# A ring of weights grows from two rounds of experts to three, and each engine reads the number of extra rounds earlier

## The chip, the cores and the metric

The kernel runs on one core of a Trainium2 chip. Its time is the device time of one execution in microseconds (us). All arithmetic is in float32. TensorE (PE) multiplies, VectorE (DVE), ScalarE (ACT) and GpSimd (POOL) do the rest, and SyncE (SP) issues the loads of the weights.

## The reference, cut to what matters

Two blocks run one after the other on 256 tokens of width 1,024. The first is one hybrid layer (three kinds of attention, then experts of hidden width 512); the second is two layers of another kind with experts of hidden width 256. Each of the three layers ends in a routed mixture: 32 experts in 4 groups, each token goes to 2 of them.

```python
x, xc = hybrid_layer(x, xc, ...)           # attention part, then hier_moe: 32 experts, 1024 -> 2*512 -> 1024
x = rms_norm(x, final_g)
for l in range(2):
    x = hybrid_layer_2(x, ...)             # mixers, then hier_moe_2: 32 experts, 1024 -> 2*256 -> 1024
out = rms_norm_2(x, final_g_2)

# an expert, for the tokens that chose it
g, u = split(h @ w_up[e]); y = (silu(g) * u) @ w_down[e]
```

The weights of the experts are 6 MiB for each expert of the first layer and 3 MiB for each of the others, so that 192, 96 and 96 MiB are read once; this is nearly all of the memory traffic.

## The kernel before, in words

**Stages.** A dense part (modulation, projections, attention, out-projection, norm, router) is followed by an expert stage, three times: stage 1 for the first layer, stages 2 and 3 for the layers 0 and 1 of the second block. Each engine has one program in order, and semaphores tie them together.

**Rounds.** An expert stage is a run of rounds. A main round takes one expert in stage 1 (32 rounds) and two in stages 2 and 3 (16 rounds each), with at most 32 tokens for an expert. An expert with more tokens has extra rounds ahead of its main round; they use the same weights, and only the main round gives the weights' memory back. How many there are depends on the routing, so it is a number in SBUF (`extra`), which every engine reads into a register (`value_load`, L913). `each_round` (L905) holds the loop. On TensorE one turn of it has two rounds, each with a body for an extra round (skipped by a branch when there is none, L914) and a body for the main round; on ScalarE and VectorE a turn has one.

A round on TensorE is, in this order: turn the gates (L965), up-projection (`up`, L987 in stage 1, L999 later; 64 matmul instructions), gather the tokens of the next round (L947), combine the result of the last one (`combine`, L974), transpose the hidden values (L1038), give slots back (L1041), transpose the gathered tokens (L954), down-projection (`down`, L1017 or L1010), and after a main round wait for its end and give back the other slots (L1049). ScalarE applies SiLU (L1077), copies the gathered tokens (L1071), the hidden values (L1080) and the result (L1082). VectorE marks the tokens of the next round (L1137, L1107), multiplies (L1142), and copies (L1146, L1126).

**Ring.** Weights arrive in a ring of `RING = 12` slots of 1 MiB (2,048 floats on each of 128 partitions). A round has `ROUND = 6` pieces: four of the up-projection and two of the down-projection. Dense layers use the same ring with pieces that take two slots each. TensorE counts used slots in `piece_used`; SP waits for the count before it loads a slot again (`expert_loads`, L446 to L461), in the order of use:

```python
sp.wait_ge(sems["piece_used"], turn * len(sources) + (base + j - RING + 1))
...
sp.dma_start(dst, src).then_inc(sem, 16)
```

So ahead of a stage two rounds can be in the ring.

**The other memory.** The activations of the dense layers lie in `arena` (18,944 columns) and in `hT` (4,096). The semaphore `mixed` says that all mixers of a layer have finished; the out-projection, the norm and the router follow it. The table `const2` of the second block is loaded once by POOL (L1192), after `fin_x`, the end of the first block.

Of the kernel before, what the change touches and what calls it, by code (L numbers as in the profile page):

```python
# [16 lines left out]
I32 = mybir.dt.int32  # L17
ALU = mybir.AluOpType
# [3 lines left out]
P = 128  # L22
# [5 lines left out]
RING = 12  # L28
ROUND = 6
NE = 32  # L30
# [125 lines left out]
SEMS = """params loaded_x loaded_ctx loaded_bias bias_out piece0 piece1 piece2 piece3 piece4 piece5 piece6 piece7 piece8 piece9 piece10 piece11 piece_used  # L156
# [42 lines left out]

class Ring:  # L200


    def __init__(self, sems):
        self.sems, self.n, self.loads = sems, 0, [0] * RING

    def place(self, dmas):

        slot = self.n % RING
        self.n += 2
        self.loads[slot] += 16 * dmas  # L210
        return slot, self.sems[f"piece{slot}"], self.loads[slot]

    def loop(self, turns, per_turn):

        out = []
        for j in range(per_turn):
            slot = (self.n + j) % RING
            out.append((slot, self.sems[f"piece{slot}"], self.loads[slot] + 16 * (j // RING + 1)))
        step = 16 * (per_turn // RING)
        self.loads = [n + step * turns for n in self.loads]  # L220
        self.n += turns * per_turn
        return out, step
# [20 lines left out]
def hybrid_kernel(nc, ins, out):  # L243
# [6 lines left out]
    with ExitStack() as ctx:  # L250
# [5 lines left out]

        ring = sb("ring", RING * SLOT).rearrange("p (r n) -> p r n", r=RING)

# [6 lines left out]
        hTf = sb("hT", KD * 2 * S)  # L265
        hT = hTf.rearrange("p (k n) -> p k n", k=KD)
        h2T = hTf[:, 0:KD * S].rearrange("p (k n) -> p k n", k=KD)
# [18 lines left out]
        arena = sb("arena", 18944)  # L286
# [7 lines left out]
        cxf = area(2048)  # L294
        rotf = area(1536)
        cx = cxf.rearrange("p (t d) -> p t d", t=NT)
        rot_b, rot_o = rotf[:, 0:512], rotf[:, 512:1536].rearrange("p (b n) -> p b n", b=2)
        qk = arena[:, 0:3584].rearrange("p (d n) -> p d n", d=2)
        q_pad = rotf[:, 0:512].rearrange("p (b m n) -> p b m n", b=2, m=2)
        probs1 = cxf.rearrange("p (b m n) -> p b m n", b=2, m=2)  # L300
        qaT = area(1024).rearrange("p (h n) -> p h n", h=4)
        kaT = area(2048).rearrange("p (h n) -> p h n", h=4)
        va = area(2048).rearrange("p (t n) -> p t n", t=4)
        vbn = area(2048).rearrange("p (t n) -> p t n", t=4)
# [4 lines left out]
        rT = area(512).rearrange("p (h n) -> p h n", h=2)  # L309
        glow = area(512)  # L310
        nb_biasf = area(2048)
        nb_bias = nb_biasf.rearrange("p (t h n) -> p t h n", t=2, h=4)
        const1 = area(n_c1)
        C1 = {n: const1[:, a:a + w] for n, (a, w) in c1.items()}
        mixf = area(2048)
        mixT = mixf.rearrange("p (k n) -> p k n", k=KD)
        wdec = area(256)[0:32, :].rearrange("p (d n) -> p d n", d=2)
# [18 lines left out]
        band_flat = arena[0:GRID, 3584:7168]  # L336
        band = band_flat.rearrange("p (r u) -> p r u", u=P)

        work = arena[:, 0:3584]
# [8 lines left out]
        junk = arena[:, 3584:4608]  # L348
        router_w = kaT.rearrange("p h n -> p (h n)")[:, 0:288].rearrange("p (k n) -> p k n", k=KD)
        rt = kaT.rearrange("p h n -> p (h n)")[:, 288:2048]  # L350
# [9 lines left out]
        extra = ctx.enter_context(nc.sbuf_tensor("extra", [1, NE], I32))  # L360
        zeros = rt[:, 960:1088]
        extra_m = rt[0:1, 1088:1104]
        final_g = va.rearrange("p t n -> p (t n)")[:, 0:D]
        vbf = vbn.rearrange("p t n -> p (t n)")
# [3 lines left out]
        junk2 = arena[:, 2560:3584]  # L368
# [4 lines left out]
        const2 = lie(7680, n_c2)  # L373
        C2 = {n: const2[:, a:a + w] for n, (a, w) in c2.items()}
        low = 7680 + n_c2
# [11 lines left out]
        st_e = work[:, 0:1536].rearrange("p (m n) -> p m n", m=2)  # L387
        st_s = work[:, 1536:3072].rearrange("p (m n) -> p m n", m=2)
        q_tok = work[:, 0:1536].rearrange("p (t h n) -> p t h n", t=NT, h=8)
        k_tok = work[:, 1536:3072].rearrange("p (t h n) -> p t h n", t=NT, h=8)  # L390
        v2 = lie(4608, 1024).rearrange("p (t h n) -> p t h n", t=NT, h=8)
        cqT = lie(5632, 768).rearrange("p (c n) -> p c n", c=3)
        q2T = hTf[:, 0:2048].rearrange("p (h n) -> p h n", h=8)
        k2T = hTf[:, 2048:4096].rearrange("p (h n) -> p h n", h=8)
        probs2 = lie(3584, 1024).rearrange("p (b m n) -> p b m n", b=2, m=2)
# [53 lines left out]
        def expert_loads(sp, plan, sources):  # L449

            base, turns, rounds = plan.n, sources[0].shape[0], len(sources) // ROUND
            slots, _ = plan.loop(turns, len(sources))
            with sp.Fori(0, turns) as turn:
                for j, (src, (slot, sem, _)) in enumerate(zip(sources, slots)):

                    sp.wait_ge(sems["piece_used"], turn * len(sources) + (base + j - RING + 1))
                    src = src[bass.ds(turn, 1)][0]
                    dst = ring[:, slot, :]
                    if len(src.shape) == 3:
                        dst = dst.rearrange("p (k n) -> p k n", k=src.shape[1])  # L460
                    sp.dma_start(dst, src).then_inc(sem, 16)  # L461

        def first_sources():

            up = ins["w_expert_up"][0].rearrange("(g e) (k p) n -> e g p k n", e=GROUP, p=P)
            down = ins["w_expert_down"][0].rearrange("(g e) (k p) n -> e g p k n", e=GROUP, p=P)
            out = []
            for e in range(GROUP):
                out += [up[e][:, :, 2 * i:2 * i + 2, :] for i in range(4)]
                out += [down[e][:, :, 2 * i:2 * i + 2, :] for i in range(2)]  # L470
            return out

        def second_sources(layer):

            gate, up = (ins[n][layer].rearrange("g (b e) (p k) n -> e (g b) p (k n)", e=GROUP, p=P)
                        for n in ("w_gate_2", "w_up_2"))
            down = ins["w_down_2"][layer].rearrange("g (b e) (k p) n -> e (g b) p k n", e=GROUP, p=P)
            out = []
            for e in range(0, GROUP, 2):
                out += [gate[e], up[e], gate[e + 1], up[e + 1], down[e], down[e + 1]]  # L480
            return out
# [331 lines left out]
        def route_dve(dve, at, link, which):  # L813
# [76 lines left out]
            if which == 1:  # L890
                link(dve.tensor_copy(extra[:, 0:NE], extra_f))
# [12 lines left out]
        def each_round(eng, at, which, per_turn, round_):  # L904
# [3 lines left out]
            n_rounds = NE // experts_of(which)  # L908
            eng.wait_ge(*at("ranked"))
            with eng.Fori(0, n_rounds // per_turn) as turn:  # L910
                for i in range(per_turn):
                    own = turn * per_turn + i
                    n = eng.value_load(extra[0:1, bass.ds(own, 1)], min_val=0, max_val=7)  # L913
                    with eng.If(n > 0):  # L914
                        with eng.Fori(0, n):
                            round_(turn, i, own, False)
# [1245 lines left out]
```

## Time and profile before

| | us |
|---|---|
| median of the 3 runs | 1,779.96 (1,773.75 to 1,780.94) |
| the profiled execution | 1,768.81 |
| its span | 1,767.0 |
| PE busy in it | 1,406.7 (80%) |
| PE weight loads | 742.5 (42%) |
| DVE, ACT, POOL busy | 452.1, 396.7, 41.7 |
| mean granted clock of PE | 0.897 |
| read from memory | 474.71 MB, 270 GB/s over the span |

A busy share is a mean over stages with different limits, and PE's matmuls overlap each other, so 80% doesn't say that PE is the bound. The page of the profile also cuts the span into 40 slices of 44.2 us each, which show the stages apart. The chain that ended last is followed back from the last instruction: at each step to what released it. "issue" in it is time in which the engine waited for nothing that the profile shows, such as reads of registers, branches and the fetch of code.

### The profile page before, as it was taken

How to read it: one execution, taken by the hardware profiler on the slowest of the kernel's cores; microseconds unless marked ns; L12 is line 12 of the kernel's file. 1: busy time of each engine (PE TensorE's matmuls, PEld its weight loads, DVE VectorE, ACT ScalarE, POOL GpSimd, SP SyncE). 2: the span in 40 equal slices, each digit the busy share in tenths (PEclk: the TensorE clock that was granted, in tenths of full speed). 3: DMA queues.
4: the chain of work that ended last, by engine and by line, in shares of the span. 5: the costliest groups of instructions: out<-in, count | busy, mean ns of one | idle time of the engine just before them, and what ended most of it. 6: DMA issues, size and time to landing. Idle time of an engine off the chain costs nothing.

```text
span 1767.0 us, 31246 instructions
## 1 busy us (share of the span) xinstructions
PE 1406.7 (80%) x12322; PEld 742.5 (42%) x12323; DVE 452.1 (26%) x1372; ACT 396.7 (22%) x766; POOL 41.7 (2%) x80
## 2 busy tenths in 40 slices
PE   3999988867777787798968878877789887998874
PEld 2555454443333343354546544333337534333331
DVE  0103346442111121122234522111123513121112
ACT  1101214112211121122223311222132412222221
POOL 2000201000000000000000000000000000000000
PEclk9999969978988898899979888989899887999897
DMA  9957300119999999969783125999992220779994
GB/s 325 341 193 286 89 31 0 63 61 397 410 410 410 409 410 410 410 255 410 286 335 143 53 95 224 418 417 417 418 354 101 96 76 36 286 305 418 417 418 176
DMA packets 125615, 477.40 MB, mean 270 GB/s; under 512 B 8977, under 2 KB 19470, under 8 KB 108990
## 3 DMA queue, kind: packets, MB, share of 16 engines
q1 hardware_dynamic: 122496, 468.61, 67.3%
q0 software_dynamic: 2160, 6.51, 1.3%
q10 hardware_dynamic: 910, 1.59, 0.3%
q8 instruction: 35, 0.57, 0.1%
q14 instruction: 14, 0.11, 0.0%
HBM read 474.71 MB, written 1.97 MB: 270 GB/s over the span
## 4 chain that ended last, share of the span: by engine, by line
PE 53%; DMA 19%; SPq 11%; issue 6%; DVE 6%; ACT 2%; PEld 2%; ACTq 0%; PEldq 0%; POOL 0%; DVEq 0%
DMA ring<-in_w_up 11%; SPq L461 10%; PE psum L1664 5%; PE psum L673 5%; PE psum L987 5%; PE psum L999 4%; DMA ring<-in_w_expert_up 4%; PE psum L974 4%; PE psum L947 3%; PE psum L1660 3%; PE psum L1017 2%; PE psum L1010 2%; DMA ring<-in_w_expert_down 2%; PE psum L1221 2%; PE psum L1233 2%
## 5 line engine op out<-in xcount | busy, mean ns | idle before, releaser
L987 PE MATMUL psum<-ring,arena 128*32 128x256 f32 x2624 | 195.9, 447 | 39.8 <-DMA ring<-in_w_expert_up 39.6
L999 PE MATMUL psum<-ring,arena 128*32 128x256 f32 x2432 | 162.4, 426 | 30.9 <-DMA ring<-in_w_up 30.7
L1142 DVE TENSOR_TENSOR arena<-arena,psum 128x128 f32<-128x128 f32 x79 | 22.8, 288 | 576.3 <-ACT arena L1077 576.3
L987 PEld LDWEIGHTS psum<-ring,arena 128*32 128x32 f32 x2624 | 86.1, 124 | 134.0 <-DMA ring<-in_w_expert_up 71.0
L999 PEld LDWEIGHTS psum<-ring,arena 128*32 128x32 f32 x2432 | 94.7, 122 | 88.5 <-issue 58.3
L974 PE MATMUL psum<-arena 32*128 32x256 f32 (+1 forms) x992 | 127.6, 469 | 2.1 <-ACT arena L1082 2.1
L947 PE MATMUL psum<-xn,arena 128*32 128x256 f32 (+1 forms) x992 | 125.8, 473 | 0.0
L965 PE MATMUL psum<-const_sb,arena 128*128 128x128 f32 x158 | 33.6, 295 | 115.2 <-issue 115.2
L1077 ACT ACTIVATE arena<-psum 128x128 f32<-128x128 f32 x79 | 21.9, 278 | 397.7 <-PE psum L987 221.7
L1077 ACT ACT_TABLE_LOAD x79 | 101.4, 1283 | 39.2 <-issue 38.9
L1664 PE MATMUL psum<-ring,hT 128*128 128x512 f32 x224 | 97.7, 593 | 0.0
L1017 PE MATMUL psum<-ring,arena 128*32 128x256 f32 x1312 | 81.5, 383 | 11.3 <-DMA ring<-in_w_expert_down 4.0
L974 PEld LDWEIGHTS psum<-arena 32*128 32x128 f32 (+1 forms) x992 | 57.9, 184 | 72.3 <-issue 67.0
L673 PE MATMUL psum<-ring,arena 128*128 128x512 f32 x192 | 85.9, 606 | 2.4 <-DVE arena L649 1.5
L965 PEld LDWEIGHTS psum<-const_sb,arena 128*128 128x128 f32 x158 | 16.1, 142 | 165.0 <-issue 165.0
L1146 DVE COPY arena<-psum 128x256 f32<-128x256 f32 x79 | 33.5, 425 | 191.1 <-ACT arena L1080 191.1
L1082 ACT ACTIVATE arena<-psum 128x256 f32<-128x256 f32 (+1 forms) x79 | 38.5, 487 | 170.9 <-PE psum L1017 91.5
L1010 PE MATMUL psum<-ring,arena 128*32 128x512 f32 x608 | 73.1, 598 | 1.2
L947 PEld LDWEIGHTS psum<-xn,arena 128*32 128x32 f32 (+1 forms) x992 | 43.2, 127 | 59.8 <-issue 48.3
L1071 ACT ACTIVATE arena<-psum 128x256 f32<-128x256 f32 (+1 forms) x82 | 40.0, 488 | 117.2 <-PE psum L947 117.2
L1664 PEld LDWEIGHTS psum<-ring,hT 128*128 128x128 f32 x224 | 41.9, 190 | 50.5 <-issue 50.5
L673 PEld LDWEIGHTS psum<-ring,arena 128*128 128x128 f32 x192 | 36.9, 194 | 50.2 <-issue 50.2
(326 smaller groups left out, 1528.8 us busy)
## 6 DMA issues: line engine op xcount, KB each, us to landing
ring<-in_w_expert_up SPq DMA_DIRECT2D x128, 1024.0 KB, 18.2
ring<-in_w_expert_down SPq DMA_DIRECT2D x64, 1024.0 KB, 18.2
ring<-in_w_gate SPq DMA_DIRECT2D x64, 1024.0 KB, 16.1
ring<-in_w_up SPq DMA_DIRECT2D x64, 1024.0 KB, 18.0
ring<-in_w_down SPq DMA_DIRECT2D x64, 1024.0 KB, 20.4
ring<-in_w_mod SPq DMA_DIRECT2D x12, 2048.0 KB, 14.6
ring<-in_w_in SPq DMA_DIRECT2D x6, 2048.0 KB, 10.2
ring<-in_w_out SPq DMA_DIRECT2D x6, 2048.0 KB, 13.2
```

The costliest lines, as they stand in the source:

```text
L461: sp.dma_start(dst, src).then_inc(sem, 16)
L673: mm = pe.matmul(ps[2 * t + n], mix[:, 4 * j + k, P * t:P * t + P], w[:, k, 512 * n:512 * n + 512], start=(j == 1 and k == 0), stop=(j == ...
L947: mm = pe.matmul(G[w * j:w * j + w, 0:wide], sel[:, t, 0:w], xn[:, t, wide * j:wide * j + wide], start=(t == 0), stop=(t == NT - 1))
L965: mm = pe.transpose(U[:, S + P * t:S + P * t + P], sel_gate[:, t, :], ident)
L974: mm = pe.matmul(out_, comb[r, P * t:P * t + P], y_sb[r, 0:S * at_once], start=False, stop=True, skip_group_check=True)
L987: mm = pe.matmul(out_(j), chosen_rows(k, 0), wt[:, kk, :, j, :], start=(k == 0), stop=(k == KD - 1))
L999: mm = pe.matmul(out_(j), chosen_rows(k, e), wt, start=(k == 0), stop=(k == KD - 1))
L1010: mm = pe.matmul(Y[quadrant(j), :], hidT[:, W * src:W * src + W], pair[e][:, half, 512 * n:512 * n + 512], start=(half == 0), stop=(half = ...
L1017: mm = pe.matmul(Y[quadrant(j), 0:S], hidT[:, W * k:W * k + W], wt[:, kk, S * j:S * j + S], start=(k == 0), stop=(k == 3))
L1077: act.activation(silu_sb, U[:, 0:P], ACT.Silu).then_inc(sems["w_silu"], 1)
L1660: mm = pe.matmul(bank[0:m, 0:tokens], w[:, k, col + P * i:col + P * i + m], hT[:, k, 0:tokens], start=(k == 0), stop=(k == KD - 1))
L1664: mm = pe.matmul(bank, hT[:, k, P * i:P * i + P], w[:, k, :], start=(k == 0), stop=(k == KD - 1))
```

## The change

- `RING` becomes 18. The first 12 slots (`HOME`) are as before. The six new ones lie in memory that the dense layers use until `mixed`: `store` holds both, and `arena` begins where slot 12 does. `hT`, the projections, `const1` and, in the second block, `const2` and its neighbours lie in the third round's slots; what is alive in an expert stage or between `mixed` and the stage (h2T, the router's values, `work`) lies behind them.
- SP loads three rounds ahead of a stage; the third waits for `mixed`. Dense pieces go through the 12 home slots alone. The loop of loads has three rounds a turn, and what is left over (2 rounds in stage 1, 1 in the others) stands behind the loop.
- TensorE's loop has three rounds a turn too (six bodies), with 2 or 1 more rounds written out behind it.
- Each engine reads the number of extra rounds for the next expert in the middle of its main round and keeps it in a register (`next_extra`), where it was read between rounds before. On TensorE the place is after `combine`, on ScalarE after the copy of the gathered tokens, on VectorE after the marks. `extra` has one more element for the read in the last round.
- `const2` and `pool_w` are loaded again in layer 1 of the second block, after the end of stage 2 (`moe_mm`), and two engines wait for that load.

```diff
-RING = 12
+HOME = 12
+RING = 18
 ROUND = 6
+TURN = RING // ROUND
...
-        ring = sb("ring", RING * SLOT).rearrange("p (r n) -> p r n", r=RING)
+        store = sb("store", HOME * SLOT + 23040)
+        ring = store[:, 0:RING * SLOT].rearrange("p (r n) -> p r n", r=RING)
+        arena = store[:, HOME * SLOT:]
...
+    def stage(self, rounds):
+        first = self.pos // 3
+        stage = Stage(self, rounds, (first, 1 - first, 2))
...
+        self.pos = 0 if self.last[0] < self.last[ROUND] else 3
+        return stage
...
+            for r in range(TURN):
+                if r == TURN - 1:
+
+                    sp.wait_ge(sems["mixed"], dense_done)
+                for j, src in enumerate(sources):
+                    sp.wait_ge(sems["piece_used"], max(stage.last[stage.slot(r, j)], 1))
+                    load(r, j, src[r])
+            turns = stage.rounds // TURN - 1
             with sp.Fori(0, turns) as turn:
...
+                for i in range(TURN):
+                    for j, src in enumerate(sources):
+
+                        sp.wait_ge(sems["piece_used"], turn * RING + (stage.base + ROUND * i + j + 1))
+                        load(i, j, src[bass.ds(turn * TURN + (TURN + i), 1)][0])
+            for r in range(TURN * (turns + 1), stage.rounds):
...
+        def next_extra(eng, name, own):
+
+            place = slice(own, own + 1) if isinstance(own, int) else bass.ds(own, 1)
+            eng.reg_mov(windows[name + "_more"], eng.value_load(extra[0:1, place], min_val=0, max_val=7))
...
+            next_extra(eng, name, 0)
+
+            def one(turn, i, own):
+
+                n = eng.snap(more)
+                with eng.If(n > 0):
+                    with eng.Fori(0, n):
+                        round_(turn, i, own, False)
+                round_(turn, i, own, True)
...
-                    n = eng.value_load(extra[0:1, bass.ds(own, 1)], min_val=0, max_val=7)
...
                 combine()
+                if last:
+                    next_extra(pe, "pe", own + 1)
                 pe.wait_ge(sems["w_hid"], v)
...
-            each_round(pe, at, which, 2, round_)
+            each_round(pe, "pe", at, which, TURN, round_)
...
-            pool.wait_ge(*at("fin_x"))
-            pool.dma_start(const2, ins["const2"]).then_inc(sems["const2"], 16)
             for layer in range(2):
+
+                pool.wait_ge(sems["moe_mm"], 1 + layer)
+                if layer == 0:
+                    pool.wait_ge(*at("fin_x"))
+                pool.dma_start(const2, ins["const2"]).then_inc(sems["const2"], 16)
```

## Rows read from the trace of the kernel before

**Rows 1.** The page, 40 slices of 44.2 us: GB/s that the DMA engines moved.

```profile
GB/s 325 341 193 286 89 31 0 63 61 397 410 410 410 409 410 410 410 255 410 286 335 143 53 95 224 418 417 417 418 354 101 96 76 36 286 305 418 417 418 176
```

**Rows 2.** Busy time by stretch, four stretches of the three expert stages.

```profile
core 0: us, PE busy (x) PEld busy (x) DVE busy (x) ACT busy (x) POOL busy (x), PEclk, DMA share, GB/s
445.00:751.00 306.00, 224.63 (x2853) 104.23 (x2843) 49.76 (x192) 55.43 (x107) 0.00 (x0) 0.86 1.03 410
844.00:858.00 14.00, 13.70 (x228) 7.74 (x231) 3.97 (x15) 4.39 (x8) 0.00 (x0) 1.00 0.07 17
1082.00:1306.00 224.00, 179.14 (x1673) 78.39 (x1671) 37.30 (x133) 48.89 (x82) 0.00 (x0) 0.94 1.02 415
1574.00:1738.00 164.00, 130.88 (x1192) 58.32 (x1192) 26.26 (x93) 35.52 (x58) 0.00 (x0) 0.92 1.02 418
```

**Rows 3.** The chain that ended last, stage 2: start us, us, what.

```profile
1221.40 22.07 DMA ring<-in_w_up
1251.81 21.78 DMA ring<-in_w_up
```

**Rows 4.** The same chain, end of stage 1; L987 x64 is one up-projection.

```profile
734.90 18.35 DMA ring<-in_w_expert_down
...
771.66 3.59 PE psum L987 x64
...
780.12 3.59 PE psum L987 x64
...
788.25 1.49 issue
...
790.16 3.59 PE psum L987 x64
...
895.39 0.39 ACT arena L1082
```

**Rows 5.** The same chain, end of stage 2; L999 x64 is one up-projection.

```profile
1273.72 3.66 PE psum L999 x64
...
1284.09 3.59 PE psum L999 x64
...
1294.06 1.44 issue
...
1295.91 3.59 PE psum L999 x64
```

**Rows 6.** PE's timeline, stage 3; in brackets idle time before, and its releaser.

```profile
1489.45 3.66 PE L999 MATMUL psum<-ring,arena 128*32 128x256 f32 x64
...
1511.60 3.66 PE L999 MATMUL psum<-ring,arena 128*32 128x256 f32 x64
...
1629.41 5.35 PE L999 MATMUL psum<-ring,arena 128*32 128x256 f32 x64 [0.98 <-DMA ring<-in_w_up]
```

**Rows 7.** One main round of stage 2: first the chain, PEq being PE's sequencer.

```profile
1189.12 0.06 PEldq L1041
```

**Rows 8.** PE's timeline of the same main round.

```profile
1190.21 1.99 PE L974 MATMUL psum<-arena 64*128 64x512 f32 x8
```

**Rows 9.** The chain, first turns of stage 1 (three rows) and of stage 2.

```profile
387.13 4.28 issue
391.40 0.66 PE psum L965 x2
...
401.32 6.57 issue
...
1073.07 5.35 PE psum L999 x64
...
1084.80 1.67 issue
```

**Rows 10.** DMA issues: KB, median us from issue to landing.

```profile
arena<-in_const POOLq DMA_DIRECT2D x1, 1216.0 KB, 8.7
```

**Rows 11.** The page, DMA queues: packets, MB, share.

```profile
q8 instruction: 35, 0.57, 0.1%
```

More of the change, by code:

```diff
@@ L197, in plus, with __init__, slot, landed @@
         return self.sems[name], self.n[name] + k
+class Stage:
+    def __init__(self, plan, rounds, order):
+        self.rounds, self.order = rounds, order
+        self.base, self.loads, self.last = plan.n, list(plan.loads), list(plan.last)
+        self.sems = plan.sems
+    def slot(self, i, j):
+        return ROUND * self.order[i] + j
+    def landed(self, turn, i, j):
+        slot = self.slot(i, j)
+        return self.sems[f"piece{slot}"], turn * 16 + (self.loads[slot] + 16)
 class Ring:
     def __init__(self, sems):
-        self.sems, self.n, self.loads = sems, 0, [0] * RING
+        self.sems, self.n, self.pos = sems, 0, 0
+        self.loads, self.last = [0] * RING, [0] * RING
     def place(self, dmas):
-        slot = self.n % RING
+        slot = 2 * self.pos
+        self.pos = (self.pos + 1) % (HOME // 2)
+        free = max(self.last[slot:slot + 2])
         self.n += 2
+        self.last[slot:slot + 2] = [self.n, self.n]
         self.loads[slot] += 16 * dmas
[L211 to L222, printed above, removed]
+        return slot, self.sems[f"piece{slot}"], self.loads[slot], free
+    def stage(self, rounds):
+        first = self.pos // 3
+        stage = Stage(self, rounds, (first, 1 - first, 2))
+        for r in range(rounds):
+            for j in range(ROUND):
+                slot = stage.slot(r % TURN, j)
+                self.n += 1
+                self.last[slot] = self.n
+                self.loads[slot] += 16
+        self.pos = 0 if self.last[0] < self.last[ROUND] else 3
+        return stage
 DMAS = {"mod": 1, "win": 1, "wout": 1, "win2": 1, "mla": 2, "wout2": 1}
@@ L473, in second_sources @@
+        def first_sources():
+            up = ins["w_expert_up"][0].rearrange("e (k p) n -> e p k n", p=P)
+            down = ins["w_expert_down"][0].rearrange("e (k p) n -> e p k n", p=P)
+            return [up[:, :, 2 * i:2 * i + 2, :] for i in range(4)] + [down[:, :, 2 * i:2 * i + 2, :] for i in range(2)]
         def second_sources(layer):
-            gate, up = (ins[n][layer].rearrange("g (b e) (p k) n -> e (g b) p (k n)", e=GROUP, p=P)
+            gate, up = (ins[n][layer].rearrange("g (b e) (p k) n -> e (g b) p (k n)", e=2, p=P)
@@ L476, in second_sources @@
                         for n in ("w_gate_2", "w_up_2"))
[L477 to L481, printed above, removed]
+            down = ins["w_down_2"][layer].rearrange("g (b e) (k p) n -> e (g b) p k n", e=2, p=P)
+            return [gate[0], up[0], gate[1], up[1], down[0], down[1]]
@@ L935, in experts_pe, with slot_ready @@
             blocks = wide // P
-            slots, step = plan.loop(NE // at_once // 2, ROUND * 2)
-            def slot_ready(turn, j):
-                slot, sem, value = slots[j]
-                pe.wait_ge(sem, turn * step + value)
-                return ring[:, slot, :]
+            stage = plan.stage(NE // at_once)
+            def slot_ready(turn, i, j):
+                pe.wait_ge(*stage.landed(turn, i, j))
+                return ring[:, stage.slot(i, j), :]
             def gather():
@@ L992, in up @@
                     for piece in range(4):
-                        slot_ready(turn, ROUND * i + piece)
-                    first = slots[ROUND * i][0]
+                        slot_ready(turn, i, piece)
+                    first = stage.slot(i, 0)
                     for k in range(KD):
@@ L1004, in down @@
                 if which == 2:
-                    pair = [slot_ready(turn, ROUND * i + 4 + e).rearrange("p (k n) -> p k n", k=2) for e in range(2)]
+                    pair = [slot_ready(turn, i, 4 + e).rearrange("p (k n) -> p k n", k=2) for e in range(2)]
                     for half in range(2):
@@ L1253, in second_block_pe @@
                 pe.wait_ge(*at("p2_v"))
-                if layer == 0:
-                    pe.wait_ge(sems["const2"], 16)
+                pe.wait_ge(sems["const2"], 16 * (1 + layer))
                 for g in range(4):
```

177 lines of the change are left out of this document (88 added, 89 removed).

## The prediction

> **What bounds the kernel now.** I read the 40 slices first. Three long stretches stand at 409 to 418 GB/s, and between them the rate falls to two digits [rows 1]. By the code these are the expert stages: stage 1 (about 390 to 895 us, 32 rounds), stage 2 (1,073 to 1,318) and stage 3 (1,489 to 1,750), 16 rounds each. A round of weights is six 1 MiB pieces, 6.29 MB: 15.35 us at 410 GB/s, 15.05 us at 418 [rows 2]. The chain of what ended last shows the same: in stage 2 it runs through one landing after another, 30.4 us apart for two rounds [rows 3].
>
> The stages are not bound by the transfers to their ends. A slot is refilled only when its main round has used it, and an extra round (an expert with more than 32 tokens) uses weights without freeing any. There are 79 rounds, 64 main and 15 extra: 9, 2 and 4 by stage, as the gaps below tell them. After extras the 12 slots are full, the DMA rests (17 GB/s at 844 to 858) and TensorE, at a granted clock of 1.00 there, sets the pace; in the long DMA-bound stretches it waits and shows 0.86 to 0.94 [rows 2].
>
> *End of stage 1:* the last binding landing is at 753.25 (734.90 + 18.35). From there TensorE alone walks through 16 rounds, 8 main and 8 extra, to 895.4: an extra costs 8.46 us (771.66 to 780.12), a main round 10.04 (780.12 to 790.16), since a main round is followed by 1.49 us in which nothing is waited for [rows 4]. *End of stage 2:* the last binding landing lets an up-projection start at 1,273.72; then come extra, main (11.8 us), extra, main [rows 5]. *Stage 3* is the other way round: it begins with four pairs of extra and main, 22.2 us a pair (1,489.45 to 1,511.60), slower than the transfer, and only from 1,629.41 on does each round wait for weights, to the last one [rows 6].
>
> **The change, part by part.**
>
> *Third round preloaded.* While the dense layers run, the DMA idles: 31, 0 and 63 GB/s in slices 6 to 8, similar before stages 2 and 3 [rows 1]. The six new loads stand in SP's queue behind the second round's, whose last four pieces wait for the out-projection's slots. So nothing new starts before the out-projection ends (355, 1,038, 1,454 us), when the DMA has 4 MiB or less plus 6 MiB to move, 25 us at 418 GB/s, against 35 us before the first round; the third is wanted two rounds later. The `mixed` wait that SP now holds is long done then. The preload is hidden, and in each stage one round less lies between the first freed slot and the last landing.
>
> - Stage 1: the landing at 753.25 moves 15.35 us up. Can a later one bind? With three rounds of slots the loads for the next two rounds go on beside the four extras; the load after them waits for slots freed at about 767 and lands at about 783, its turn is at about 802. The last round's load starts at about 838 and lands at 854, its turn is at about 870. Nothing binds; the full 15.35 us come through.
> - Stage 2: 1,273.72 moves up by 15.05. The last round's weights come 15.05 us later, its turn 21.4 (an extra, a main less the read). 15.05 us.
> - Stage 3: the DMA line starts when the fourth main round frees its slots, and 10 rounds follow it where 11 did: 15.05 us.
>
> *The read in the middle of a main round.* Before, each engine reads the count between two rounds. On TensorE this stands after the wait for the last down-projection, so its queue is empty and the read is bare. The gap behind a main round is 1.44 to 1.49 us, and none shows behind an extra [rows 4, 5]. It holds the wait, the read and two branches; the read's share is no row. It is worth between 0 and 1.49 us; I take 0.75, half, as the wait and branches stay. In the middle, TensorE's sequencer is ahead: it passes L1041, which stands behind the read's new place, at 1,189.12, while the L974 matmuls that stand before it start at 1,190.21 and last 1.99 us [rows 7, 8]. So 3 us of queued matmuls cover it; uncovered it would cost its 0.75 again. On ScalarE and VectorE it falls ahead of waits of theirs and costs nothing; uncovered, 0.75 each, but neither sets the pace. The saving counts only where TensorE does: 7 main-to-next steps at the end of stage 1 (5.3 us), one in stage 2 (0.75), three before the DMA line of stage 3 (2.25). What is queued behind the read on TensorE is the release of slots (`piece_used`, four at once in stages 2 and 3): 0.75 us later, and so the DMA lines of stages 2 and 3 start 0.75 later. Net: stage 1 5.3, stage 2 0, stage 3 1.5.
>
> *The loop over three rounds.* On TensorE the loop now holds six bodies instead of four, and behind it stand two more main and two more extra bodies in stage 1, one and one in stages 2 and 3. Entering fresh code costs: in the first turn of stage 1 the two skips over an extra body stand as 4.28 and 6.57 us of issue [rows 9], against 1.49 later, so 2.8 and 5.1. The new skips: one at the third round of stage 1 (it delays release of its slots by up to 5, but the DMA has some 4 us of backlog then: 1 us), two behind the loop of stage 1, both in the stretch where TensorE sets the pace, 0 to 5.1 each; I take 2.5 each, as the place of the skip in the code decides, 5 us in all. In stage 3 the one skip lies where TensorE has 3.8 us to spare a round, in stage 2 the last round has an extra and nothing is skipped: 0. ScalarE's and VectorE's loops keep their length. SP's code, 18 loads a turn instead of 24 or 12, has a 2.5 us transfer behind each issue as cover.
>
> *The rest.* Layer constants lie where the third round goes, so they are loaded again in layer 1, after stage 2's end, with POOL's queue waiting for `moe_mm`; behind that wait are only pool_w and the router's weights. The 1.2 MB landed 8.7 us after issue [rows 10], with weights moving too; first use is over 25 us after the stage's end: 0, and if cover were gone at most some 10 us. Addresses of hT, h2T, qk, work and the others move, instructions and shapes stay: 0. The reuse of the order of slots lets the first dense pieces of layer 1 start a round earlier: 0, as no dense matmul there waits for weights.
>
> **Sum.** Stage 1: 15.35 + 5.3 - 1 - 5 = 14.7. Stage 2: 15.05. Stage 3: 15.05 + 1.5 = 16.6. Together 46 us less. The profiled execution took 1,768.8 us (span 1,767.0 and 1.8 around it): 1,722.5. The median of the runs, 1,780.0, is 11 us above that execution; from it I would come to 1,733.7. I predict 1,729.
>
> **Rivals.**
>
> *The read stalls TensorE where it now stands* (if it must find the queue empty). For: no row shows such a read among queued matmuls. Against: the sequencer's lead [rows 7, 8]. Each of the 11 steps then costs 0.75 more instead of less: 46 - 8 - 8 = 30 us, 1,745.
>
> *The third round is no use*: its loads come only when the stage has begun, or the late rounds are bound by TensorE anyway. For: the TensorE-bound ends of stages 1 and 2 [rows 4, 5]. Against: their start is set by a landing, which moves. Only reads less code are left, 1 to 8 us: 1,770 to 1,775, no difference that 0.5% (about 9 us, what a measurement of this kernel can tell) shows.
>
> *The longer loop no longer stays loaded* and every skip pays what the first turn pays. This one ends slower. Before, fetches of code were 35 in the whole run, 0.57 MB [rows 11], for 79 rounds with over 200 loads and matmuls each: a repeated loop of four bodies is not fetched again. Six could be too many. With a stall s per main round TensorE would take, to the end of stage 1, 391 [rows 9] + 9 x 8.46 + 32 x (9.29 + s) = 764 + 32s, against 895 now; stage 2, 1,073 + 2 x 10.4 + 16 x (11.1 + s) = 1,271 + 16s against 1,318; stage 3, 1,489 + 4 x 10.4 + 16 x (11.1 + s) = 1,708 + 16s against 1,750. The three sum to 220 us less plus 64s: slower from s = 3.4 us on. At the 5.1 us of the first turn it would be 106 us slower, 1,880 from the mean of both bases. Against it as well: in stage 2, whose bodies are a quarter shorter, the first turn shows only 1.67 us where 1.44 is usual [rows 5, 9].
> The Trainium skill (Runtime: NRT & Kernel Launch, "Instruction fetch mechanics") gives TensorE room for 2,048 instructions, fetched in blocks of 256, and says that a taken branch out of the window must fetch its target before going on. By its figure, estimated with 276 instructions to a stage 1 body, six bodies are 1,656 and stay in, so this rival would not come; the 35 fetches for the loop of four agree.
>
> *More than forecast:* no stall behind stage 1's loop and a read worth 1.49: 46 + 6 + 8 = 60 us, 1,714.
>
> **How the numbers follow.** Forecast (gain 38 to 55) 0.58; more 0.09; stalled read 0.20; third round of no use 0.05; code reloaded 0.08, of which a little still ends faster through small s. Faster by over 0.5%: 0.58 + 0.09 + 0.20 + 0.01 = 0.88; within 0.5%: 0.05; slower: 0.07. The range goes from 1,709 (60 us off the mean of both bases is 1,714, less 5 for the scatter of runs, which span 7 us) to 1,755 (a stalled read from the higher base, 1,750, and scatter). What lies above it are the last two cases.
>
> **What the profile after would show.** Right: in stage 2 the last up-projection that waits for a landing starts near 1,244 (1,258.7 less the 14.7 of stage 1), landings still 30 us apart for two rounds; a burst of 6 MiB between out-projection and first round; the last landing of stage 1 that binds near 739; behind a main round an issue gap of about 0.75 instead of 1.49, and none new between L974 and the transposition behind it; two issue gaps of up to 6 us just before stage 1's end. Wrong: fetches of code far above 35 with issue gaps in every turn; landings that bind no earlier than before; a wait for const2 in layer 1; a lower granted clock in the stretches where TensorE sets the pace.

## The result, and the profile after

The changed kernel takes 1,844.3 us (median of 4, 1,842.2 to 1,854.0) against 1,776.9 (median of 4, 1,770.1 to 1,780.9): 1.0402 times as long, interval 1.037 to 1.0434. That is 67 us slower where I had forecast 46 us less. The rival that I had given 0.08, the longer loop that no longer stays loaded, came in stage 1, and in stage 1 alone.

The page, with the rows that answer to [rows 1] and [rows 11] (slices of 46.1 us here), and the clock that TensorE was granted:

```profile
PEclk8899969968788787779798889789989988899998
GB/s 330 313 182 273 115 1 1 162 222 361 339 391 356 339 322 367 348 342 108 306 210 314 103 108 89 233 379 418 418 418 333 101 82 207 141 299 358 418 417 205
q8 instruction: 129, 2.11, 0.5%
```

Two things differ at a glance. Stage 1, which stood at 410 GB/s for eight slices, now moves between 322 and 391 in the nine full slices. Fetches of code are 129 instead of 35, each of 16 KB. They have times of their own in the trace. Of the 129, 91 start between 392 and 998, in stage 1, and 6 in each of the other two stages; the kernel before has 3 in its stage 1 and none from 425 us on. Queue 8 between 392 and 998, and in the turn of TensorE's loop looked at below (432 to 487):

```profile
q8 instruction: 91, 1.49, 1.1%
q8 instruction: 9, 0.15, 1.3%
```

Stages 2 and 3 still reach 418 GB/s. Part 4 of the page, the shares of the chain that ended last by engine, says the same: issue is 15% of it, and was 6%; DMA fell from 19% to 8%.

Busy time by stretch, the three expert stages whole and, first, one turn of TensorE's loop in stage 1 (three rounds); columns as in [rows 2]:

```profile
435.00:489.50 54.50, 30.93 (x399) 15.65 (x399) 7.02 (x27) 7.82 (x15) 0.00 (x0) 0.78 0.89 348
392.00:998.00 606.00, 388.06 (x5395) 204.01 (x5397) 93.49 (x360) 104.32 (x201) 0.00 (x0) 0.82 0.81 314
1181.00:1407.00 226.00, 192.47 (x1819) 82.68 (x1821) 37.77 (x139) 51.78 (x87) 0.00 (x0) 0.94 0.96 388
1584.00:1816.00 232.00, 205.89 (x2022) 90.81 (x2021) 42.03 (x155) 57.62 (x95) 0.00 (x0) 0.98 0.86 352
```

Stage 1 does the same work, 5,395 matmuls busy for 388 us; the same stage of the kernel before has 5,393 and 390 us, in 499 us instead of 606. So TensorE has not become slower at its work; it stands still more. The turn takes 54.5 us where the transfers of three rounds want 46.05 (three times 15.35), so the DMA engines now wait for TensorE (share 0.89). What TensorE waits for is in the chain of the same turn (L1041 is the up-projection, L1071 the down-projection, L1019 the turning of the gates with which a round begins):

```profile
432.17 14.19 issue
446.36 0.66 PE psum L1019 x2
447.02 6.31 PE psum L1041 x64
...
457.87 6.42 issue
...
464.95 5.88 PE psum L1041 x64
...
475.44 1.25 issue
...
477.10 3.59 PE psum L1041 x64
...
486.66 14.04 issue
```

None of the waits in the code ends these gaps: each stands where one round has ended and the next can start. The 14.19 us hold the branch back to the loop's start and the skip over its first extra body, the 6.42 the skip over the second, the 1.25 the skip over the third, and with 14.04 the next turn begins. In the kernel before, this gap was 1.49 us within a turn [rows 4] and 1.82 at its end. Fetches of code start in both long gaps: four in the 14.19 us and one in the 6.42. After the two long gaps the up-projection also takes 6.31 and 5.88 us instead of 3.59. The granted clock, by stretch, of the 14.19 us gap, of these two up-projections and of the third:

```profile
432.17:446.36 14.19, 0.00 (x1) 0.03 (x1) 0.11 (x2) 1.67 (x2) 0.00 (x0) 0.62 0.96 376
447.02:453.33 6.31, 6.31 (x68) 2.98 (x72) 0.00 (x0) 0.00 (x0) 0.00 (x0) 0.57 0.47 166
464.95:470.83 5.88, 5.88 (x68) 2.83 (x72) 0.00 (x0) 0.00 (x0) 0.00 (x0) 0.61 0.66 235
477.10:480.69 3.59, 3.59 (x68) 2.17 (x72) 0.00 (x0) 0.20 (x1) 0.00 (x0) 1.00 1.03 418
```

A mean of 0.57 or 0.61 is mostly the lower of the clock's two levels (1.2 of 2.4 GHz); TensorE had done nothing for 14.19 and 6.42 us before. Over the whole turn the granted clock is 0.78. One round shows what the stall hangs on. Where an extra round is executed, TensorE runs on into its body instead of skipping it, and the gap ahead of it is 0.74 us in the same place of the loop (the second round of a turn) where a skip takes 6.42:

```profile
672.98 0.74 issue
673.72 0.41 PE psum L1019 x2
674.13 3.59 PE psum L1041 x64
```

The gaps repeat all through the stage: each of the nine branches back to the start of the loop stands as 12.7 to 14.5 us, and the waits by total, count and longest agree (in the kernel before they are 115.2 us, longest 6.6):

```profile
PE psum L1019 <- issue: 213.9, 41, 14.5
```

Stage lengths, read from the timelines of the profiled executions (first up-projection to start of the last SiLU; us), for all kernels of this study. What lies outside the three stages takes 774 to 790 us in every kernel, 780 before and 779 after:

| kernel | span | stage 1 | stage 2 | stage 3 | code fetches |
|---|---|---|---|---|---|
| before | 1,767.0 | 498.8 | 236.8 | 251.2 | 35 |
| after | 1,842.4 | 605.6 | 225.3 | 232.1 | 129 |
| e1_one_body | 1,718.7 | 479.7 | 225.2 | 240.0 | 36 |
| e2_read_only | 1,763.8 | 493.8 | 238.6 | 249.0 | 35 |
| e3_stage1_two_rounds | 1,720.7 | 491.3 | 222.7 | 232.1 | 41 |
| e4_padding_552 | 1,971.9 | 701.0 | 236.9 | 251.1 | 135 |
| e5_one_body_early | 1,707.6 | 479.7 | 221.5 | 231.7 | 36 |
| e6_ring12_one_body | 1,787.4 | 508.7 | 242.0 | 254.4 | 29 |
| e7_padding_276 | 1,776.8 | 502.0 | 236.8 | 252.0 | 36 |
| e8_padding_416 | 1,782.4 | 504.9 | 236.9 | 253.9 | 36 |
| e9_padding_484 | 2,002.8 | 724.9 | 237.1 | 251.2 | 141 |
| e10_early_read_between | 1,719.4 | 481.9 | 220.5 | 237.0 | 36 |

After against before: stage 1 106.8 us longer, stage 2 11.5 and stage 3 19.1 shorter, together 76.2 more; the span is 75.4 longer. So the forecast held in two stages and was turned round in one.

### The profile page after: what moved, and what is told of

It reads as the page before. It is cut to its first block, busy times and chain, and to the rows that moved or that the text cites. A ratio compares the mean times of both kernels' runs of the same rounds, so it can differ in the third digit from the quotient of the medians.

```text
span 1842.4 us, 31390 instructions
## 1 busy us (share of the span) xinstructions
PE 1397.4 (76%) x12322; PEld 744.3 (40%) x12323; DVE 450.5 (24%) x1373; ACT 396.6 (22%) x766; POOL 42.6 (2%) x81
## 4 chain that ended last, share of the span: by engine, by line
PE 66%; issue 15%; DMA 8%; DVE 6%; ACT 2%; SPq 1%; PEld 0%; ACTq 0%; POOL 0%; PEldq 0%; DVEq 0%
PE psum L1041 10%; DMA store<-in_w_up 6%; PE psum L1053 6%; PE psum L1028 6%; PE psum L1001 5%; PE psum L1725 5%; PE psum L713 5%; PE psum L1071 4%; PE psum L1064 3%; PE psum L1721 3%; PE psum L1019 2%; PE psum L1284 2%; PE psum L1296 2%; PE psum L559 1%; PE psum L593 1%
## 5 line engine op out<-in xcount | busy, mean ns | idle before, releaser
L1019 PE MATMUL psum<-const_sb,store 128*128 128x128 f32 x158 | 37.3, 322 | 233.9 <-issue 213.9
L1041 PE MATMUL psum<-store 128*32 128x256 f32 x2624 | 192.3, 456 | 3.7 <-issue 3.7
L1053 PE MATMUL psum<-store 128*32 128x256 f32 x2432 | 155.2, 409 | 29.4 <-DMA store<-in_w_up 22.9
L1001 PE MATMUL psum<-xn,store 128*32 128x256 f32 (+1 forms) x992 | 126.9, 458 | 9.0 <-issue 9.0
L1019 PEld LDWEIGHTS psum<-const_sb,store 128*128 128x128 f32 x158 | 17.4, 155 | 283.6 <-issue 283.6
L1041 PEld LDWEIGHTS psum<-store 128*32 128x32 f32 x2624 | 94.2, 130 | 91.3 <-issue 58.1
L1133 ACT ACTIVATE store<-psum 128x128 f32<-128x128 f32 x79 | 21.9, 278 | 503.0 <-PE psum L1041 343.5
L1028 PE MATMUL psum<-store 32*128 32x256 f32 (+1 forms) x992 | 127.6, 469 | 1.9 <-ACT store L1140 1.9
L1053 PEld LDWEIGHTS psum<-store 128*32 128x32 f32 x2432 | 88.9, 117 | 84.4 <-issue 49.9
L1725 PE MATMUL psum<-store 128*128 128x512 f32 x224 | 97.7, 593 | 0.0
L1028 PEld LDWEIGHTS psum<-store 32*128 32x128 f32 (+1 forms) x992 | 57.9, 184 | 71.7 <-issue 66.6
L713 PE MATMUL psum<-store 128*128 128x512 f32 x192 | 83.8, 594 | 2.5 <-DVE store L689 1.5
L1071 PE MATMUL psum<-store 128*32 128x256 f32 x1312 | 79.8, 382 | 7.1 <-ACT store L1138 3.1
L1140 ACT ACTIVATE store<-psum 128x256 f32<-128x256 f32 (+1 forms) x79 | 38.4, 487 | 164.3 <-PE psum L1071 85.6
L1064 PE MATMUL psum<-store 128*32 128x512 f32 x608 | 73.1, 598 | 0.7
L1001 PEld LDWEIGHTS psum<-xn,store 128*32 128x32 f32 (+1 forms) x992 | 41.6, 120 | 70.4 <-issue 56.9
L1127 ACT ACTIVATE store<-psum 128x256 f32<-128x256 f32 (+1 forms) x82 | 40.0, 488 | 128.7 <-PE psum L1001 128.7
L1725 PEld LDWEIGHTS psum<-store 128*128 128x128 f32 x224 | 41.9, 190 | 50.5 <-issue 50.5
L713 PEld LDWEIGHTS psum<-store 128*128 128x128 f32 x192 | 36.1, 190 | 48.8 <-issue 48.8
## 6 DMA issues: line engine op xcount, KB each, us to landing
store<-in_w_expert_down SPq DMA_DIRECT2D x64, 1024.0 KB, 10.5
store<-in_w_gate SPq DMA_DIRECT2D x64, 1024.0 KB, 14.9
```

The lines of the kernel that those rows point to most:

```text
L713: mm = pe.matmul(ps[2 * t + n], mix[:, 4 * j + k, P * t:P * t + P], w[:, k, 512 * n:512 * n + 512], start=(j == 1 and k == 0), stop=(j == ...
L1001: mm = pe.matmul(G[w * j:w * j + w, 0:wide], sel[:, t, 0:w], xn[:, t, wide * j:wide * j + wide], start=(t == 0), stop=(t == NT - 1))
L1019: mm = pe.transpose(U[:, S + P * t:S + P * t + P], sel_gate[:, t, :], ident)
L1028: mm = pe.matmul(out_, comb[r, P * t:P * t + P], y_sb[r, 0:S * at_once], start=False, stop=True, skip_group_check=True)
L1041: mm = pe.matmul(out_(j), chosen_rows(k, 0), wt[:, kk, :, j, :], start=(k == 0), stop=(k == KD - 1))
L1053: mm = pe.matmul(out_(j), chosen_rows(k, e), wt, start=(k == 0), stop=(k == KD - 1))
```

## The experiments

The gaps lie where TensorE skips a body, and the loop has six bodies now. Two things were to be told apart: that the length of the loop makes the stall, or that something else of the change does (memory that has moved, the third round's loads, the read among queued matmuls). And the parts that were forecast as gains were to be measured without the stall.

**One body for both kinds of round (e1).** On TensorE the extra round and the main round become turns of one inner loop, so that three rounds are three bodies instead of six and nothing is skipped. The price: in this form all six slots of a round are given back at its end.

```diff
+                if name == "pe":
+                    with eng.Fori(0, n + 1) as again:
+                        round_(turn, i, own, (again, n))
+                    eng.wait_ge(sems["w_y"], eng.snap(windows["pe"]))
+                    eng.sem_inc(sems["piece_used"], ROUND)
+                    return
...
-                        if last and piece < 3:
-                            mm.then_inc(sems["piece_used"], 1)
...
-                if last:
-                    next_extra(pe, "pe", own + 1)
+                next_extra(pe, "pe", own + 1)
```

> The changed kernel, with one body per round on TensorE in place of two: the body runs in a loop of (extra rounds + 1), and all six slots are given back after it. TensorE's loop of three rounds then has three bodies instead of six. Theory A (TensorE's loop of six bodies does not stay loaded in stage 1, each turn is fetched again): no stalls of 6 and 14 us in stage 1, fetches of code back to about 35, stage 1 below the 503 us of before, and the whole at 1,730 to 1,745, the later release of slots taking some 4 us a stage of the gain. Theory B (the third round of slots itself, its place in memory, or the read in the middle of a round stalls stage 1): stage 1 stays near 610 us, the whole at 1,830 to 1,850.

Measured: 1,720.6 us, ratio 0.9687 (0.9662 to 0.9712). Stage 1 takes 479.7 us, 125.9 less than in the kernel after, and fetches of code are back at 36. Everything else of the change is in this kernel: ring of 18, store, reads in mid-round (on TensorE now in extra rounds too). None of these makes the loss.

**The read alone (e2).** The kernel before with only the earlier reads on the three engines.

```diff
                 combine()
+                if last:
+                    next_extra(pe, "pe", bass.ds(own + 1, 1))
                 pe.wait_ge(sems["w_hid"], v)
...
-                    n = eng.value_load(extra[0:1, bass.ds(own, 1)], min_val=0, max_val=7)
+                    n = eng.snap(more)
```

> The kernel before, ring of 12 and loop of two rounds, with the read of the next count moved to the middle of a main round on all three engines. Theory A: the read is covered there; behind a main round the gap shrinks by about 0.75 us, worth 8 us in all: 1,769, ratio 0.995. Theory B (the read stalls TensorE among queued matmuls): gaps between L974 and the transposition, 1,780 to 1,850 depending on the stall.

Measured: 1,765.2 us, ratio 0.9918 (0.9896 to 0.9939), 12 us less than before by the medians; by the profiled spans only 3.2: stages 1 and 3 give 5.0 and 2.2, and stage 2 and the dense parts lose 1.8 and 2.2. The chain of one stretch at the end of stage 1 (L981 is `combine`, L1047 the transposition, L1091 ScalarE's copy of the hidden values):

```profile
786.64 1.08 PE psum L981 x16
787.72 0.27 PE psum L1047
788.00 0.02 issue
788.02 0.29 ACT arena L1091
...
790.33 0.79 issue
...
799.73 1.26 issue
```

Both gaps of this stretch stand behind main rounds, 0.79 within a turn and 1.26 at its end. The kernel before has 1.49 [rows 4] and, at the end of the turn, 1.82 in its chain:

```profile
798.37 1.82 issue
```

So the read's share is 0.70 and 0.56. The transposition (L1047), which stands right behind the read, starts as the last matmul of `combine` ends (786.64 + 1.08), with nothing between them. The rival of a stalled TensorE is out.

**Two rounds a turn in stage 1 (e3).** The change whole, but with TensorE's and SP's loops over two rounds in stage 1, so through the 12 home slots alone; stages 2 and 3 keep three.

```diff
+        stage = Stage(self, rounds, (first, 1 - first, 2), 2 if rounds == NE else TURN)
```

> The changed kernel, but stage 1 uses two rounds of slots (12) and a loop of two rounds; stages 2 and 3 keep 18 slots and three rounds. Theory A: stage 1 as before (about 500 us, no stalls of 6 and 14 us), stages 2 and 3 as in the changed kernel, 11 and 19 us shorter than before: 1,740 to 1,748. Theory B with the memory's place as cause: stage 1 stays longer than before by tens of us. Theory B with the number of slots as cause: same as theory A, so this run tells the place from the loop only.

Measured: 1,730.8 us, ratio 0.974 (0.9719 to 0.976). Stage 1 takes 491.3 us with four bodies in the loop, stages 2 and 3 keep their gains (14.1 and 19.1 us). The activations lie where they lie in the kernel after, so their place doesn't make the loss, and the six new slots were in e1.

**Only code added (e4, e7, e8, e9).** The kernel before, with instructions behind the second main round of a turn of stage 1 that are never executed: a branch that is never entered. One such matmul is four instructions, as the 32 in the code of an up-projection stand in the trace as 64 matmuls and 64 loads, so 138 of them are 552 instructions, about two bodies.

```diff
                     round_(turn, i, own, True)
+                    if which == 1 and eng is PE and i == per_turn - 1:
+                        with eng.If(n > 6):
+                            for _ in range(138):
+                                eng.matmul(ps[0][:, 0:P], ident, ident, start=True, stop=True)
```

> The kernel before, with 138 matmuls (552 instructions) added at the end of TensorE's loop of stage 1 behind a branch that is never taken: nothing more is executed, the loop is only as long in code as that of the changed kernel. Theory A: fetches of code well above 35, stalls of 6 us and more in every turn of stage 1, 1,800 to 1,880. Theory B: as before, 1,777.

Measured: 1,973.7 us (one execution), 196 more than the 1,777.7 of the kernel before beside it; 135 fetches, 103 of them in stage 1. The chain of one turn has the picture of the kernel after, with the long gap where the padding is skipped and the loop goes back:

```profile
495.55 18.90 issue
...
515.12 4.66 PE psum L992 x64
...
524.32 6.47 issue
...
531.46 5.02 PE psum L992 x64
...
541.09 2.18 issue
```

This is the direct evidence: nothing that is executed, moved or loaded differs from the kernel before but one skip a turn, and the stall is there. But not in every turn: the one that follows begins after 2.18 us. Of the 15 branches back, read as idle time of TensorE, 11 stand as 16.6 to 21.6 us, the first as 8.0 and three as 2.1 to 2.2. A turn is two rounds here and 16 turns pass, against three rounds and 10 turns, so the loss is larger than the change's own.

Three more sizes sought the edge, with 69, 104 and 121 matmuls in the branch:

> As the padded kernel, with 69 matmuls (276 instructions) behind the branch: TensorE's loop of stage 1 is some 1,400 instructions long, near the 1,330 of the changed kernel's stages 2 and 3, which were not fetched again. If only the length of the loop decides: as before, 1,770 to 1,782, some 36 fetches. If a skip over 276 instructions by itself costs: 16 turns of 3 to 6 us, part of it hidden, 1,790 and more.

> The same with 104 matmuls (416 instructions), a loop of some 1,540. Between the length that stays (1,330) and one that doesn't (1,676 with 552 of padding, 1,974 us): either about 1,777 or about 1,950, nothing between, if a loop that is one block too long is fetched as a whole in every turn.

> The kernel before with 121 matmuls (484 instructions) behind the branch that is never taken, a loop of some 1,600 instructions in stage 1. With 416 the time was 1,784 and 36 fetches were seen, with 552 it was 1,974 and 135. The theory says either some 36 fetches and about 1,785, or about 135 and 1,900 to 1,980, with nothing between; which of the two says where between 1,540 and 1,676 the edge lies.

Measured: 1,778.6, 1,784.2 and 2,004.6 us (one execution each). The page of e8 and the page of e9:

```profile
q8 instruction: 36, 0.59, 0.1%
```

```profile
q8 instruction: 141, 2.31, 0.5%
```

With 416 instructions stage 1 is 6.1 us longer than before and has no fetch after its first turns (none from 432 us on); 68 more cost 220 us and bring 110 fetches into the stage. A body of stage 1 has 266 loads and matmuls (399 of each in three) and by the code about 14 waits, increments and branches (the trace of the turn above has 46 such for three), 280 in all. The loop with 416 more is 4 x 280 + 416 = 1,536 and was kept, the one with 484 more is 1,604 and was not; six bodies are 1,680. In stage 2, 3,640 loads and matmuls over 18 rounds are 202 each, with the 14 others 216, and six bodies about 1,300: kept, and stages 2 and 3 show no gaps once their first turn is over. Between the two there is no slope: one shows no fetch once it runs, the other has 12 of its 15 branches back at 16.5 to 21.9 us. Length is not all of it, though: three branches back of e9 take 2.2 us, as in e4, and e9 took 31 us longer than e4 with less padding. How the code lies against the fetched pieces of 16 KB may matter too; it was not varied by itself. The exact edge between 1,536 and 1,604 was not sought.

**Early release with one body (e5).** As e1, but four of the six slots are given back behind the transposition, as in stages 2 and 3 of the kernel after, under a test for the last inner turn.

```diff
+                again, n_extra = last
+                with pe.If(again == n_extra):
+                    pe.sem_inc(sems["piece_used"], 4)
...
-                    eng.sem_inc(sems["piece_used"], ROUND)
+                    eng.sem_inc(sems["piece_used"], 2)
```

> The one-body kernel, but four of a round's six slots are given back behind the transposition of the hidden values, under a branch that is taken in the main round alone, and two at its end. If the later release costs the one-body kernel what its stages 2 and 3 lack against the changed kernel with two rounds in stage 1 (225 and 240 us against 223 and 232), this gets 5 to 10 us back: 1,711 to 1,716. The rival: the added branch breaks the sequencer's lead in the middle of the round and costs 0.3 to 0.7 us a round where TensorE sets the pace: 1,721 to 1,728.

Measured: 1,710.1 us, ratio 0.9634 (0.9608 to 0.9661), the fastest kernel of the study, 10.5 us below e1. Stage 1 doesn't change against e1 (479.7 both), stages 2 and 3 give 3.7 and 8.3. Its page:

```profile
GB/s 330 324 234 296 60 65 1 1 261 286 410 410 409 410 410 410 410 386 366 310 360 99 99 118 232 418 417 418 417 341 154 148 66 197 209 290 418 418 417 190
q8 instruction: 36, 0.59, 0.1%
```

The last landing of stage 1 that sets the pace, in its chain, answers to the one of [rows 4]:

```profile
713.79 18.20 DMA store<-in_w_expert_up
731.99 0.04 issue
...
782.95 0.67 issue
```

It comes at 731.99, 21.3 us before the 753.25 of the kernel before. The gap behind a main round is 0.67 us.

**Ring of twelve with one body (e6).** e2 and e1's inner loop, without the third round.

```diff
+                    if name == "pe":
+                        with eng.Fori(0, n + 1):
+                            round_(turn, i, own, True)
+                        eng.wait_ge(sems["w_y"], eng.snap(windows["pe"]))
+                        eng.sem_inc(sems["piece_used"], ROUND)
+                        continue
```

> The kernel before (12 slots, two rounds a turn) with the read in the middle and one body per round. Against the one-body kernel with 18 slots (1,721) it leaves out the third round alone. Theory: the third round is worth one round's transfer a stage, 15 us each, so 1,764 to 1,768, or up to 1,775 as the later release hurts a ring of 12 more. The rival: the third round is worth little and the gain of the one-body kernel came from the short loop: 1,720 to 1,735.

Measured: 1,782.3 us, ratio 1.0038 (1.0017 to 1.006), above the range that was expected. Against e2 the late release of slots costs 17.1 us by the medians and 23.6 by the profiled spans. Against e1 the difference is the third round, with the memory and the loads that it needs, and it is worth 61.6 us by the medians; by the profiled executions 29.0, 16.8 and 14.4 in the three stages. In stages 2 and 3 that is about the transfer of one round; in stage 1 it is 13.7 us more than one. There the late release costs 14.9 us with 12 slots (508.7 against 493.8 in e2) and nothing with 18 (479.7 in e1 and in e5), so a third round also hides it.

**The read between rounds, in the best version (e10).** e5 with `next_extra` at the start of `one()` on all engines.

```diff
             def one(turn, i, own):
 
+                next_extra(eng, name, own)
                 n = eng.snap(more)
...
-                next_extra(pe, "pe", own + 1)
```

> The one-body kernel with the early release (1,710) with the read of the count put back between the rounds on all three engines. If the read in the middle is covered and its saving holds in this kernel too, this is 8 to 15 us slower, 1,718 to 1,725, as the read alone gave 0.8% in the kernel before. The rival: with three rounds of slots the saving is hidden behind the transfers: within 4 us of 1,710.

Measured: 1,718.3 us, ratio 0.9675 (0.9655 to 0.9696), 8.1 us above e5. Stages 1 and 3 take 2.2 and 5.3 us longer, stage 2 1.0 less. The waits (total, count, longest) of e5 and, below, of e10 show the gap before a round:

```profile
PEld psum L1025 <- issue: 103.3, 79, 2.0
```

```profile
PEld psum L1025 <- issue: 149.7, 79, 2.8
```

46.4 us more over 64 main rounds are 0.73 us a read. Only 8.1 of them show in the time; the rest, it seems, falls where TensorE waits for weights anyway.

## Why the prediction was wrong

**The step that failed** is "The loop over three rounds". I costed the six bodies at two entries into fresh code behind the loop and one at the third round, 6 us, and took from the 35 fetches of a loop of four bodies that a loop of six would stay loaded too. That doesn't follow: 35 fetches show that some 1,120 instructions are kept and tell nothing of 1,680. A row that bears on the question was missing, and in its place the chance of 0.08 rested on a page: the Trainium skill (Runtime: NRT & Kernel Launch, "Instruction fetch mechanics") gives 2,048 instructions as room. The runs here disagree: a loop of about 1,604 was fetched again in every turn. That section also says that a taken branch whose target isn't loaded must wait for its fetch. The trace of e4 agrees: five fetches start within the 18.90 us in which the padding is skipped and the loop goes back, and the padding itself is never executed.

**The rival's arithmetic** held better than its chance. 764 + 32s gives the measured end, 998, for s = 7.3 us a round; that is fitted, and I had set 5.1 from the first turn. Read off the turn above: 54.5 us less three unhindered rounds of 9.29 are 26.6 us, of which the three gaps over 0.75 each are 19.6 and the two slow up-projections 5.0; 8.9 a round where no extra round comes between. The entry into fresh code in the first turn was too low a price, as the branch back costs 14 us and a skip 6.4. Where it failed was the break-even: it assumed that all stages would stall, and they differ by body length, which I had noted for stage 2 and not used. Stage 1 alone sufficed to turn a gain of 31 us into a loss.

**The third round:** right in mechanism and, in stages 2 and 3, in size. 15.05 each were forecast there, and 15.35 for stage 1. e6 and e1 differ by 16.8 and 14.4 in stages 2 and 3; the 29.0 of stage 1 hold the late release as well. In e5, which has the whole change with three bodies in TensorE's loop instead of six, the stages are 19.1, 15.3 and 19.5 shorter; my terms without the code's are 15.35 + 5.3 = 20.65, 15.05 and 16.6. In the kernel after, stage 2 came to 11.5. Its first turn shows why, in the chain:

```profile
1193.95 3.88 issue
1197.82 5.75 PE psum L1053 x37
...
1211.30 3.15 PE psum L1053 x52
1214.44 2.50 issue
```

TensorE stands still inside up-projections of rounds that it enters for the first time, before the line of transfers begins, and one fetch of code starts within each of the two gaps. e5 has no such gap there. I had looked for such stalls at skips alone and put 0 for stage 2; they are 6.4 us in two places, and the shortfall against e5 is 3.8. Later in the stage the chain goes through landings as forecast, and the gap behind a main round is 0.98 us, where 1.44 stood [rows 5]:

```profile
1346.38 22.95 DMA store<-in_w_up
...
1369.47 5.35 PE psum L1053 x64
...
1391.49 0.98 issue
```

**The read:** right in size. Forecast 0.75 saved for each main round; e2 shows 0.70 and 0.56, e10 0.73. No gap appeared between `combine` and the transposition (L981 and L1047 in e2 above). What these add up to is less sure than one of them: 3.2 us by spans and 12.5 by medians in e2, 8.1 by medians and 11.8 by spans in e10, against 6.8 in my sum (5.3 + 0 + 1.5). The scatter of runs is of that size.

**Stage 3:** right up to 2.5 us (19.1 against 16.6). The last round still waits for its weights, as forecast:

```profile
1812.27 3.83 PE L1053 MATMUL psum<-store 128*32 128x256 f32 x64 [1.75 <-DMA store<-in_w_up]
```

**The rest:** right. `const2` landed 7.7 us after issue and nobody waits for it; the dense parts between stages changed by 1.3 and 2.4 us.

```profile
store<-in_const POOLq DMA_DIRECT2D x2, 1216.0 KB, 7.7
```

**What stays open.** Why the change makes 94 fetches more in 10 turns, 9.4 a turn, where the padded loops make 6.3 (100 in 16) and 6.6 (106 in 16), was not tried, nor why three turns of each padded loop begin without a gap. Nor was the length of the gaps varied against the load on the DMA engines, which these fetches share with the weights at 322 to 391 GB/s. The release in the middle of a round is worth 10.5 us with 18 slots by e1 and e5; it was not split among the rounds.

## What to carry to other kernels

Before a loop is unrolled further, count its instructions, each engine's by themselves and skipped bodies too (only TensorE's limit was measured here), and compare with a loop that is known to stay loaded; a count of code fetches from the kernel before says that its own loop fits and nothing more, and a loop padded with a branch never entered measures the room in one run. Two bodies that differ in a few instructions, one of them mostly skipped, can be one body in an inner loop with a test around those few; without that test, and so with slots released late, one body lost 17 us in a ring of 12 (e6 against e2). A price worked out for a rare rival should be worked out stage by stage: one stage that falls can outweigh two that gain.

## What the runs showed that I had not expected

- A loop of about 1,536 instructions on TensorE is kept and one of about 1,604 is fetched again in most turns; the 68 instructions between them, which never run, cost 220 us (1,784.2 to 2,004.6).
- A turn of a loop that isn't kept has gaps of 14.2 and 6.4 us in the kernel after, 18.9 and 6.5 in e4.
- The gaps cost twice: after one an up-projection ran at a granted clock of 0.57 and took 6.31 us instead of 3.59, 5.0 of the 26.6 us that the turn shown loses. Over stage 1 the granted clock is 0.82 where it was 0.90.
- A body that is entered in order costs no such gap (0.74 us), one that is skipped does (6.42).
- Never-executed code that stays loaded costs little or nothing: with 276 and 416 instructions stage 1 was 3.2 and 6.1 us longer in one execution each, where runs of the kernel before scatter over 11 us.
- The expected sizes were missed more often than the directions: e1, e3 and e5 came out faster than their ranges (1,720.6, 1,730.8 and 1,710.1 against 1,730, 1,740 and 1,711 at least), and e4, e6 and e9 slower (1,973.7, 1,782.3 and 2,004.6 against 1,880, 1,775 and 1,980 at most).
